# Routing a mixture-of-experts layer in another tile order: prompt tile 0, the sample tile, prompt tile 1

## The chip, the cores and the metric

The kernel runs on one core of a Trainium2 chip. It is one inference step of a two-layer hybrid decoder: a prompt group of 256 tokens and a sample group of 8 sequences with 8 tokens each, 320 tokens in all, in float32. The metric is the device time of one execution in microseconds (us). A core has five engines with a queue each: TensorE (PE, matrix products; its weight loads are shown as PEld), VectorE (DVE), ScalarE (ACT), GpSimd (POOL) and SyncE (SP, which here only issues DMAs). They meet through semaphores.

## The reference, cut to what matters

Each layer is a pair of mixers, whose outputs are projected back to width 1024 and added to the residual, followed by this block (`x` is the normalised residual):

```python
def hier_moe(x, p):
    xf = x.reshape(bt * t, dm)
    g_logits = (xf @ p['router_g']) + p['router_g_b']          # 4 groups
    g_idx = jnp.argmax(g_logits, axis=-1)
    e_logits = (xf @ p['router_e'] + p['router_e_b']).reshape(n, 4, 4)
    e_in = jnp.take_along_axis(e_logits, g_idx[:, None, None], axis=1)[:, 0]
    top_v, top_i = lax.top_k(e_in, 2)                           # 2 of the group's 4 experts
    top_w = jax.nn.softmax(top_v, axis=-1) * g_w
    ...
    hid = silu(x @ w_gate) * (x @ w_up)                         # 16 experts, 1024 -> 256
    y = (hid * gates) @ w_down                                  # 256 -> 1024
```

`yp + hier_moe(rmsnorm(yp))` and the same for the samples is what the changed part computes the beginning of: projection, norm, logits, choice, and the place of every token in its expert.

## The kernel before, in words

The 320 tokens lie in three tiles: tiles 0 and 1 are the prompt (128 rows each), tile 2 is the samples (64 rows); `ROWS = (P, P, NB * NS)`. `moe_block` runs once for each of the two layers, and only its first stage, up to the first expert product, is touched. In that stage each tile goes through the same steps, which pass between the engines:

1. PE: `project(t, h)` multiplies the mixers' output by the output weights, half `h` of 512 columns, in `n_parts` products of 128x512 (8 in layer 0, 6 in layer 1; `ahead` says how many are already done). For the samples, `project_samples(first, end)` does both halves of a part side by side in bank 4. The semaphore `done` counts finished halves.
2. DVE: `add(t)` adds the product to the residual (L1815), half by half; semaphore `added`.
3. ACT: square with row sum (L1736), square root (L1739); DVE: reciprocal in `mean(t)` (L1820); ACT: the scaled rows `xn` (L1741), which are also written to DRAM as `x_rows` (L1743) for later gathers.
4. PE: `turn_rows(t)` transposes the residual (L1439); DVE: `apply_gain(t)` copies it out with the norm's gain (L1827).
5. PE: `logits(t)` (L1447), DVE: `logits_out(t)` (L1835), PE: `logits_back(t)` (L1456).
6. DVE: `choose` and `mark`, a chain of short instructions (L1873 to L1905) that finds group and experts. Tiles 0 and 1 go through it together, tile 2 after them.
7. PE: `places` counts tokens of earlier tiles in each expert (L1463), DVE: `place` turns counts into one-hot slots `Sf` (L1910, L1913).
8. PE: `gather_first(t)` collects the rows of the first pair of experts, 8 products of 128x128 for each tile (L1470); DVE: `first_turned(h)` copies them out (L1840). Meanwhile DVE computes slot codes up to `L` (L1943), and PE multiplies them (L1608) to the table of row numbers `idx` (L1949), from which POOL starts the gathers of the later pairs (L1383).
9. PE: `up(0, 0, KC)`, the first expert product (L1499), 32 records, ends the stage. Seven more pairs of experts follow.

PE, DVE and ACT each take their instructions in the order in which the code is written; there is no planner. `keep_clock_up(bank, n, cols)` (L182) issues `n` products whose result nobody reads. SP waits for `done` to reach 6, then loads the next experts' weights into the room of the output weights (L135, L142), and piece by piece follows PE after that (L1263).

## Time and profile before

| | |
|---|---|
| median of 3 runs | 589.82 us (589.1 to 590.4) |
| profiled execution, its own time | 589.97 us |
| its span, first to last instruction | 587.9 us |
| PE busy | 565.3 us, 96% |
| DVE, ACT, POOL busy | 42%, 26%, 12% |
| mean granted TensorE clock | 0.991 |
| stage in layer 0, first projection to first expert product | 114.60 to 157.97 us |
| stage in layer 1 | 430.68 to 471.47 us |

A time in the trace is read from the span's start. The span ends about 2 us short of the execution's own time. In a timeline row the first number is the start, the second the duration of the merged instructions, `xN` the number of records (a float32 product is two records, a transpose one), and the brackets give idle time of the engine before the row and who ended it. Neighbouring PE records overlap by their pipeline depth, so the next row's start says more of the pace than the duration. The busy share counts every matmul record, useful or not.

### The profile page before, as it was taken

What the parts mean: (1) busy time and instruction counts of PE and PEld (TensorE: products, weight loads), DVE (VectorE), ACT (ScalarE), POOL (GpSimd) and SP (SyncE); (2) the same over time, 40 slices, a digit from 0 to 9 for tenths busy, and PEclk for the clock granted to TensorE, in tenths of its full rate; (3) what the DMA queues carried; (4) which work ended last, traced back from release to release, by engine and by line L of the source; (5) the groups of instructions that cost most, each with busy time, mean ns of one, the idle gap of its engine ahead of it and who ended that gap; (6) DMA issues with size and microseconds to landing.
All of it is one profiled execution on the core that took longest, in us unless ns stands there. A gap on an engine that the chain in (4) does not pass through costs nothing. (4 is left out here: it accounts for less than half of the span.)

```text
span 587.9 us, 8565 instructions
## 1 busy us (share of the span) xinstructions
PE 565.3 (96%) x3454; PEld 314.5 (53%) x3454; DVE 249.7 (42%) x595; ACT 154.6 (26%) x327; POOL 70.7 (12%) x114
## 2 busy tenths in 40 slices
PE   6999999999989999999999999999999899999994
PEld 5677876543633333337877555667644643333331
DVE  6999783224642211154542514260113742221146
ACT  6132195121301011034245104254003300101113
POOL 5900800000101210000100001000000021120000
PEclk9999999999899999999999999999999989999998
DMA  8994999896999999899899998999699999999972
GB/s 326 418 348 73 225 402 381 366 413 290 364 359 414 422 420 419 353 356 385 345 414 320 412 405 309 316 347 423 253 400 417 392 350 402 423 418 422 384 239 91
DMA packets 39930, 208.95 MB, mean 355 GB/s; under 512 B 12819, under 2 KB 14547, under 8 KB 23920
## 3 DMA queue, kind: packets, MB, share of 16 engines
q1 hardware_dynamic: 30416, 169.93, 74.2%
q0 software_dynamic: 7872, 34.53, 16.3%
q10 hardware_dynamic: 1600, 3.90, 1.7%
q8 instruction: 30, 0.49, 0.3%
q14 instruction: 12, 0.10, 0.0%
HBM read 198.77 MB, written 43.74 MB: 412 GB/s over the span
## 5 line engine op out<-in xcount | busy, mean ns | idle before, releaser
L1499 PE MATMUL bank<-arena 128*64 128x512 f32 x264 | 87.0, 611 | 0.2 <-DVE arena L1840 0.2
L1499 PE MATMUL bank<-ring,arena 128*64 128x512 f32 x232 | 76.1, 614 | 0.6 <-DVE arena L1849 0.5
L2315 PE MATMUL bank<-arena,ring 128*128 128x320 f32 x256 | 71.6, 434 | 0.0
L2315 PEld LDWEIGHTS bank<-arena,ring 128*128 128x128 f32 x256 | 48.0, 190 | 21.4 <-issue 1.6
L1499 PEld LDWEIGHTS bank<-arena 128*64 128x64 f32 x264 | 24.4, 140 | 32.8 <-issue 32.6
L1420 PE MATMUL bank<-ring,arena 128*128 128x512 f32 x92 | 40.3, 594 | 1.0 <-PEq L455 0.6
L1530 PE MATMUL bank<-arena 128*64 128x512 f32 x136 | 39.8, 594 | 0.7 <-ACT arena L1754 0.7
L577 PE MATMUL bank<-xnT,ring 128*128 128x320 f32 x144 | 39.5, 434 | 0.5 <-DVE xnT L896 0.5
L1974 DVE COPY arena<-bank 128x512 f32<-128x512 f32 x14 | 9.7, 692 | 68.3 <-PE bank L1530 68.3
L1530 PE MATMUL bank<-ring,arena 128*64 128x512 f32 x120 | 36.1, 593 | 0.7 <-ACT arena L1754 0.7
L1499 PEld LDWEIGHTS bank<-ring,arena 128*64 128x64 f32 x232 | 21.7, 140 | 26.2 <-issue 26.1
L577 PEld LDWEIGHTS bank<-xnT,ring 128*128 128x128 f32 x144 | 27.1, 190 | 11.6 <-DVE xnT L896 0.7
L1752 ACT ACTIVATE arena<-bank 128x256 f32<-128x256 f32 x16 | 6.1, 384 | 95.6 <-PE bank L1499 95.6
L1968 DVE TENSOR_TENSOR arena<-arena,bank 128x256 f32<-128x256 f32 x16 | 6.7, 421 | 55.2 <-ACT arena L1752 55.2
L1420 PEld LDWEIGHTS bank<-ring,arena 128*128 128x128 f32 x92 | 17.2, 190 | 22.7 <-issue 22.7
L1849 DVE TENSOR_TENSOR arena<-bank,small 128x512 f32<-128x512 f32 x28 | 18.0, 686 | 21.7 <-PE bank L1481 21.6
L1757 ACT COPY arena<-bank 128x512 f32<-128x512 f32 x16 | 9.4, 586 | 65.0 <-PE bank L1530 65.0
L1391 POOL DMA_INDIRECT y_rows<-arena x12 | 12.1, 1007 | 107.2 <-DVE arena L1974 107.2
L1530 PEld LDWEIGHTS bank<-arena 128*64 128x64 f32 x136 | 12.4, 136 | 20.7 <-issue 20.1
L2371 PE MATMUL bank<-ring,arena 128*128 128x512 f32 (+1 forms) x64 | 21.2, 489 | 0.0
L1736 ACT ACTIVATE arena<-resid 128x1024 f32<-128x1024 f32 (+1 forms) x6 | 6.3, 1058 | 54.8 <-DVE resid L1815 54.8
L1530 PEld LDWEIGHTS bank<-ring,arena 128*64 128x64 f32 x120 | 11.3, 136 | 16.2 <-issue 15.8
(451 smaller groups left out, 849.5 us busy)
## 6 DMA issues: line engine op xcount, KB each, us to landing
arena<-in_w_moe SPq DMA_DIRECT2D x50, 1024.0 KB, 15.6
ring<-in_w_moe SPq DMA_DIRECT2D x44, 1024.0 KB, 14.4
arena<-in_stream_b SPq DMA_DIRECT2D x4, 2560.0 KB, 14.5
out_o_d_old<-in_cache_d_g POOLq DMA_DIRECT2D x1, 8448.0 KB, 29.8
arena<-in_stream_a SPq DMA_DIRECT2D x4, 2048.0 KB, 10.1
out_o_d_old<-in_cache_d_g POOLq DMA_DIRECT2D x1, 7680.0 KB, 40.6
out_o_d_old<-in_cache_d_g SPq DMA_DIRECT2D x1, 4608.0 KB, 37.7
ring<-in_w_out_even SPq DMA_DIRECT2D x2, 2048.0 KB, 11.9
```

The costliest lines, as they stand in the source:

```text
L577: last = nc.tensor.matmul(bank(name)[:, 0:TOK], lhs(k), c.xnT[:, k, :], start=(k == 0), stop=(k == KC - 1))
L1391: pool.indirect_dma_start(out=x["y_rows"], out_offset=bass.IndirectOffsetOnAxis(ap=scatter_idx[:, j:j + 1], axis=0), in_=yo_of(j), in_offs ...
L1420: last = nc.tensor.matmul(c.bank[2 * t + h][:, :], parts[q][:, t * P:(t + 1) * P], where[q][:, h * 512:(h + 1) * 512], start=(q == 0), sto ...
L1499: last = nc.tensor.matmul(c.bank[2 + j % 2][half, :], xgT[:, j % 2, q, half], w[i][q // 4][:, q % 4, :], start=(q == 0), stop=(q == KC - 1))
L1530: last = nc.tensor.matmul(c.bank[4 + h][half, :], hidT[:, j % 2, f, half], w[i][:, f, h * 512:(h + 1) * 512], start=(f == 0), stop=(f == 1))
L1736: nc.scalar.activation(xn[0:rows, t], c.resid[0:rows, t], ACT.Square, accum_out=c.stat[0:rows, t:t + 1]).then_inc(sq_ok, 1)
L1757: nc.scalar.copy(yo_of(j)[:, 0:512], c.bank[4][:, :]).then_inc(yo_a, 1)
L1849: v.tensor_tensor(xgT[:, j % 2, 4 * h:4 * h + 4, :], c.bank[h][:, :].rearrange("p (k r) -> p k r", k=4), c.gains[:, gain, 4 * h:4 * h + 4] ...
L1968: v.tensor_tensor(hid[:, j % 2], sg[:, j % 2], c.bank[2 + j % 2][:, FF:2 * FF], ALU.mult).then_inc(hid_ok, 1)
L1974: v.tensor_copy(yo_of(j)[:, 512:D], c.bank[5][:, :]).then_inc(yo_b, 1)
L2315: last = nc.tensor.matmul(bank(name)[:, 0:TOK], w[:, k, i * P:(i + 1) * P], xnT[:, k, :], start=(k == 0), stop=(k == KC - 1))
L2371: last = nc.tensor.matmul(bank(f"v{2 * t + n}")[:, 0:m], xnT[:, k, t * P:(t + 1) * P], wv[:, k, c0:c0 + m], start=(k == 0), stop=(k == KC ...
```

## The change

The order of the tiles becomes 0, 2, 1 (`ROUTED`), and all semaphore counts follow it. PE issues tile 0's two halves, then the samples' projection with tile 0's transposes and logits amid it, then tile 1's projection with tile 2's transposes, logits and the `places` of tiles 0 and 2 amid it. Tile 1's transposes go to the banks as before, tile 2's to banks 4 and 7. The first half of tile 1 is transposed before its last product, the second half after it, with three `keep_clock_up` products on both sides. On DVE `choose`, `mark` and `place` are done for one tile at a time: three chains where there were two. The gathers of tiles 0 and 2 come after the projection, tile 1's last. `first_turned(1)` moves behind `idx`. SP's first piece in layer 0 waits for `first_pe` 3 and `rows_out` too.

```diff
+ROUTED = (0, 2, 1)
+TURN_BANKS = ((0, 1), (2, 3), (4, 7))
@@ SP
             if layer == 0:
                 sp.wait_ge(first_out, 32)
-                sp.wait_ge(first_pe, 2)
+                sp.wait_ge(rows_out, 16)
+                sp.wait_ge(first_pe, 3)
@@ PE
             project(0, 0)
             project(0, 1)
-            project(1, 0)
+            project_samples(0, 2)
             turn_rows(0)
-            project(1, 1)
+            project_samples(2, 4)
             pe.wait_ge(ld, ROUTER_LOADS)
             logits(0)
-            project_samples(0, 1)
-            turn_rows(1)
+            project_samples(4, n_parts - 1)
             logits_back(0)
-            project_samples(1, 2)
+            project_samples(n_parts - 1, n_parts)
+            project(1, 0, 0, 2)
+            turn_rows(2)
+            project(1, 0, 2, 4)
+            logits(2)
+            project(1, 0, 4, 5)
+            logits_back(2)
+            project(1, 0, 5, n_parts)
+            project(1, 1, 0, 3)
+            pe.wait_ge(tri_ok, 1)
+            pe.wait_ge(sel_ok, 2)
+            places((0, 2)).then_inc(pos_pe, 1)
+            project(1, 1, 3, n_parts - 1)
+            turn_rows(1, (0,))
+            project(1, 1, n_parts - 1, n_parts)
+            c.keep_clock_up(c.bank[0], 3, 256)
+            turn_rows(1, (1,))
+            c.keep_clock_up(c.bank[0], 3, 256)
             logits(1)
-            project_samples(2, 3)
+            pe.wait_ge(S0_ok, 2)
+            pe.wait_ge(xn_ok, 2)
+            gather_first(0, 0, 2)
             logits_back(1)
...
+            gather_first(0, 2, KC)
+            gather_first(2, 0, 4)
             c.keep_clock_up(c.bank[0], 2, 256)
-            pe.wait_ge(sel_ok, 2)
-            places((2,))
+            pe.wait_ge(sel_ok, 3)
+            places((1,))
             for u in range(3):
                 last = nc.tensor.matmul(c.bank[7][:, 64:80], ones, m["sum"][:, u, :], start=(u == 0), stop=(u == 2))
             last.then_inc(pos_pe, 1)
-            pe.wait_ge(S0_ok, 2)
+            gather_first(2, 4, KC)
+            pe.wait_ge(S0_ok, 3)
             pe.wait_ge(xn_ok, 3)
-            gather_first(2)
+            gather_first(1)
@@ DVE (choose, mark and place now take one tile)
             add(0)
             mean(0)
             apply_gain(0)
-            add(1)
-            logits_out(0)
-            mean(1)
-            apply_gain(1)
...
+            logits_out(0)
+            choose(0)
+            mark(0)
+            add(2)
+            mean(2)
+            apply_gain(2)
+            logits_out(2)
+            choose(2)
+            mark(2)
+            place(0)
+            place(2)
+            add(1)
+            apply_gain(1)
+            mean(1)
             logits_out(1)
-            choose(0, 2)
-            mark(0, 2)
+            choose(1)
+            mark(1)
...
             first_turned(0)
-            first_turned(1)
 
             dve.wait_ge(idx_pe, 1)
             v.tensor_scalar(m["idx"].bitcast(U32), ...).then_inc(idx_ok, 1)
+            first_turned(1)
```

PE in layer 0, in the middle of the stage, before: the line with 64x512 is the samples' projection (L1428), L1439 a transpose, L1447 and L1456 the logits and their way back, L1463 the counts, L1470 the gather.

```order
L1420 MATMUL bank<-ring,arena 128x512 x8
L1447 MATMUL bank<-xnT,arena 20x128 x8
L1428 MATMUL bank<-ring,arena 64x512 x2
L1439 MATMUL bank<-ident,resid 128x128 x8
L1456 MATMUL bank<-small,arena 128x20
L1428 MATMUL bank<-ring,arena 64x512 x2
L1447 MATMUL bank<-xnT,arena 20x128 x8
L1428 MATMUL bank<-ring,arena 64x512 x2
L1456 MATMUL bank<-small,arena 128x20
L1428 MATMUL bank<-ring,arena 64x512 x8
L1463 MATMUL bank<-arena 128x16 x3
```

The same place after, where the lines have moved on by 3 or 4 (L1432 is the samples' projection, L1443 a transpose, L1423 tile 1's projection):

```order
L1451 MATMUL bank<-xnT,arena 20x128 x8
L1432 MATMUL bank<-ring,arena 64x512 x6
L1460 MATMUL bank<-small,arena 128x20
L1432 MATMUL bank<-ring,arena 64x512 x2
L1423 MATMUL bank<-ring,arena 128x512 x2
L1443 MATMUL bank<-ident,resid 128x64 x8
L1423 MATMUL bank<-ring,arena 128x512 x2
L1451 MATMUL bank<-xnT,arena 20x64 x8
L1423 MATMUL bank<-ring,arena 128x512
L1460 MATMUL bank<-small,arena 64x20
L1423 MATMUL bank<-ring,arena 128x512 x6
L1467 MATMUL bank<-arena 128x16 x3
```

What stood after the whole of tile 1's projection now stands amid it, and the transposes that come after the samples' projection are the samples' own, three instructions behind its end.

PE in layer 0, end of the stage, before (L1599 is the count of all tiles, L1608 the row numbers, L182 `keep_clock_up`):

```order
L1439 MATMUL bank<-ident,resid 128x64 x8
L1470 MATMUL bank<-arena 128x128 x2
L1447 MATMUL bank<-xnT,arena 20x64 x8
L1470 MATMUL bank<-arena 128x128 x2
L1456 MATMUL bank<-small,arena 64x20
L1470 MATMUL bank<-arena 128x128 x8
L182 MATMUL bank<-resid,ident 128x256 x2
L1463 MATMUL bank<-arena 128x16 x3
L1599 MATMUL bank<-arena 128x16 x3
L1470 MATMUL bank<-arena 128x128 x8
L1608 MATMUL bank<-arena 128x16 x12
L1499 MATMUL bank<-arena 64x512 x16
```

And after, from the last projection on:

```order
L182 MATMUL bank<-resid,ident 128x256 x3
L1443 MATMUL bank<-ident,resid 128x128 x4
L182 MATMUL bank<-resid,ident 128x256 x3
L1451 MATMUL bank<-xnT,arena 20x128 x8
L1474 MATMUL bank<-arena 128x128 x2
L1460 MATMUL bank<-small,arena 128x20
L1474 MATMUL bank<-arena 128x128 x10
L182 MATMUL bank<-resid,ident 128x256 x2
L1467 MATMUL bank<-arena 128x16 x3
L1598 MATMUL bank<-arena 128x16 x3
L1474 MATMUL bank<-arena 128x128 x12
L1608 MATMUL bank<-arena 128x16 x12
```

Eight unread products stand there instead of two, and between the counts and the row numbers there are twelve gather products instead of eight.

DVE in layer 0 before, from tile 0's gain (L1827) on; L1815 is the addition of tile 1:

```order
L1827 TENSOR_TENSOR xnT<-bank,small 128x4x128 x2
L1815 TENSOR_TENSOR resid<-bank,resid 128x512 x2
L1835 COPY arena<-bank 128x128
L1820 RECIPROCAL stat<-stat 128x1
L1827 TENSOR_TENSOR xnT<-bank,small 128x4x128 x2
L1861 CAST arena<-arena 128x256
```

And after, from the reading of tile 0's logits (L1871) to the samples' addition (L1816) :

```order
L1871 SCALAR_TENSOR_TENSOR arena<-bank,stat,arena 128x16
L1874 MAX arena<-arena 128x8
L1875 MAX_INDEX arena<-arena 128x8
L1876 CAST arena<-arena 128x1
L1877 TENSOR_SCALAR arena<-arena 128x16
L1878 TENSOR_TENSOR arena<-arena 128x16
L1879 MAX arena<-arena 128x8
L1880 MAX_INDEX arena<-arena 128x8
L1881 CAST arena<-arena 128x2
L1887 TENSOR_TENSOR arena<-arena 128x16 x2
L1890 TENSOR_TENSOR arena<-arena 128x16
L1816 TENSOR_TENSOR resid<-bank,resid 64x512 x2
```

The samples' addition, which PE's transposes wait for, now stands behind this whole chain of choice for tile 0.

## Rows read from the trace of the kernel before

**Rows 1.** The page, part 1: engine, busy us, share, instructions.

```profile
PE 565.3 (96%) x3454; PEld 314.5 (53%) x3454; DVE 249.7 (42%) x595; ACT 154.6 (26%) x327; POOL 70.7 (12%) x114
```

**Rows 2.** Timeline of PE, layer 0: start, us, line, operation, records, idle before.

```profile
114.60 13.97 PE L1420 MATMUL bank<-ring,arena 128*128 128x512 f32 x32 [0.60 <-PEq L455]
128.41 1.04 PE L1439 MATMUL bank<-ident,resid 128*128 128x128 f32 x8
129.28 7.03 PE L1420 MATMUL bank<-ring,arena 128*128 128x512 f32 x16
136.25 0.63 PE L1447 MATMUL bank<-xnT,arena 128*20 128x128 f32 x16
...
138.75 0.30 PE L1456 MATMUL bank<-small,arena 128*128 128x20 f32 x2
...
146.12 0.22 PE L1463 MATMUL bank<-arena 128*128 128x16 bf16 x3 [0.57 <-DVE arena L1905]
146.26 1.08 PE L1428 MATMUL bank<-ring,arena 128*64 128x512 f32 x4
...
148.85 0.70 PE L1439 MATMUL bank<-ident,resid 64*128 64x64 f32 x8 [0.42 <-DVE resid L1815]
...
151.37 2.05 PE L1470 MATMUL bank<-arena 128*128 128x128 f32 x16
153.26 1.03 PE L182 MATMUL bank<-resid,ident 128*128 128x256 f32 x4
...
155.35 2.05 PE L1470 MATMUL bank<-arena 64*128 64x128 f32 x16 [0.76 <-DVE arena L1913]
157.37 0.44 PE L1608 MATMUL bank<-arena 128*128 128x16 bf16 x12
157.97 8.63 PE L1499 MATMUL bank<-arena 128*64 128x512 f32 x32 [0.16 <-DVE arena L1840]
```

**Rows 3.** Timeline of PE, layer 1.

```profile
456.25 2.79 PE L1428 MATMUL bank<-ring,arena 128*64 128x512 f32 x12
460.22 0.22 PE L1463 MATMUL bank<-arena 128*128 128x16 bf16 x3 [1.17 <-DVE arena L1905]
...
471.47 8.78 PE L1499 MATMUL bank<-ring,arena 128*64 128x512 f32 x32 [0.16 <-DVE arena L1840]
480.19 1.09 PE L1481 MATMUL bank<-ident,arena 128*128 128x128 f32 x8
...
486.51 3.65 PE L1499 MATMUL bank<-arena 128*64 128x512 f32 x16
```

**Rows 4.** Timeline of DVE, layer 0.

```profile
125.26 0.16 DVE L1820 RECIPROCAL stat<-stat 128x1 f32<-128x1 f32 x1 [2.82 <-ACT stat L1739]
129.05 1.29 DVE L1827 TENSOR_TENSOR xnT<-bank,small 128x512 f32<-128x512 f32 x2 [3.62 <-PE bank L1439]
...
147.39 1.41 DVE L1815 TENSOR_TENSOR resid<-bank,resid 64x512 f32<-64x512 f32 x2 [0.36 <-PE bank L1428]
...
151.55 0.21 DVE L1873 SCALAR_TENSOR_TENSOR arena<-bank,stat,arena 64x4 f32<-64x4 f32 x1 [0.68 <-PE bank L1456]
...
154.06 0.17 DVE L1905 TENSOR_TENSOR arena<-arena 64x16 bf16<-64x16 f32 x1
...
154.92 0.38 DVE L1913 TENSOR_TENSOR arena<-arena 128x128 f32<-128x128 f32 x1
```

**Rows 5.** Windows of 3 us: busy by engine, then PEclk, the granted clock.

```profile
158.00:161.00 3.00, 3.00 (x8) 1.06 (x10) 1.73 (x11) 0.00 (x0) 1.17 (x2) 0.50 1.03 434
472.00:475.00 3.00, 3.00 (x10) 1.19 (x8) 1.23 (x10) 0.00 (x0) 1.72 (x2) 0.50 0.84 341
```

**Rows 6.** Layer 1: first gather, by POOL.

```profile
472.98 1.10 POOL L1383 DMA_INDIRECT arena<-x_rows,arena  x1 [3.82 <-DVE arena L1949]
```

**Rows 7.** DMAs issued from 464.0 to 464.5 us: KB, us to landing.

```profile
x_rows<-arena ACTq DMA_DIRECT2D x1, 256.0 KB, 7.0
```

## What was predicted before the changed kernel ran

> **What bounds the kernel now.** I read the page's busy shares first: PE is busy for 565.3 of 587.9 us, 96% [rows 1], so a changed stage is paid for on PE unless PE waits there. Then PE's timeline through the two routing stages. In layer 0 PE waits 0.57 us for the choice of tiles 0 and 1 (L1905), 0.42 for the samples' addition (L1815), 0.76 for the last slots (L1913) and 0.16 for the first gained rows (L1840), 1.9 us in all [rows 2]. In layer 1 the same kind of waits are 1.17 and 0.16 [rows 3], and a third like layer 0's 0.76, some 2.1 us. That is all that hiding the chain can win as waits. Third, the granted clock: it stands at 0.50 from 158 to 161 us and from 472 to 475 us [rows 5], the lower of its two levels, 1.2 instead of 2.4 GHz. Both falls come right behind the same place: the samples' gather of 64 rows, which PE waited 0.76 us for, and twelve tiny products (L1608). The first expert product runs into them and takes 8.63 us in layer 0 and 8.78 in layer 1 [rows 2, 3]. Later the same work of 16 records takes 3.65 us with its drain [rows 3], so 3.5 of pace, and 32 records would be 7.1 with drain 7.2. The falls cost 1.4 us in layer 0 and 1.6 in layer 1, 3.0 together; half of twice 3.2 us at half speed gives the same size.
>
> So two accounts are moved by the change: the length of the stage up to the start of the first expert product, and the clock behind it.
>
> **Prices.** From starts of neighbouring rows: a 128x512 product 0.86 us (13.81 us for 16); eight transposes 0.87, four 0.45; the samples' eight 0.64 from a duration of 0.70 less overlap [rows 2]. A part of the samples' projection 0.87 in a run (2.79 less drain, for 3) [rows 3], 1.0 alone; logits about 0.56, their way back about 0.22, from 0.63 and 0.30 less overlap; a tile's gather 1.89 (151.37 to 153.26), so 0.24 a product [rows 2]. A `keep_clock_up` product of 256 columns is half of a 512 one, 0.43; the row's 1.03 for two [rows 2], which ends where a wait ends, bounds it at 0.52 from above. On DVE one chain of choice and marking is 2.68 us (151.55 to 154.23), the samples' addition 1.41, two gains 1.29, one slot instruction 0.38 [rows 4].
>
> **What is added outright.** Products nobody reads: eight instead of two in layer 0 (order, end of the stage) and eight instead of four in layer 1, where the old code had two more at the samples' turn. At 0.43 each that is 2.6 and 1.7 us. All other PE work is the same in number. So even without any wait the stage would be 2.6 - 1.9 = 0.7 us longer in layer 0 and 0.4 shorter in layer 1: the stage as such has next to nothing to win, and every new wait is a loss.
>
> **Walk through layer 0.** PE starts at 114.60. Eight products to 121.5, two sample parts, tile 0's transposes, two parts: 126.2. The logits need the gained rows. The reciprocal of tile 0 starts at 125.26 [rows 4]; before, the transposes were later than that, now it is what DVE's gains stand behind: 125.4 + 1.29 = 126.7. New wait 0.6. Then logits, three parts, way back, one part, two products of tile 1: 133.1. Here PE wants to transpose the samples. Their addition stands behind tile 0's choice on DVE: logits back at 130.3, copy and semaphores 0.3, 130.55 + 2.68 + 1.41 = 134.6. New wait 1.5, the largest one. From there PE has work: transposes 0.64, two products, logits (0.1 wait for ACT's and DVE's norm), one product, way back, six products, counts at 143.9 (the samples' choice ends at 141.5, in time), four, half a transposition, one: 148.8. Before, the projection ended at 147.3 (146.26 + 1.08). So +1.5.
>
> The tail, from there to the first expert product, was 157.97 - 147.34 = 10.6. Now on PE: three unread 1.3, half the transposes 0.45, three unread 1.3, logits 0.56, two gather products 0.5, way back 0.3, ten gather products 2.4, two unread 0.9, counts 0.2, four and eight gather products 2.85, row numbers 0.4, 0.2 of wait for the first gained half: 11.4. The DVE chain in it (way back at 4.5 us, choice 2.7, counts waiting for PE until 7.9, slots 0.6, codes 1.9, gained half 0.65) ends at the same 11.4: the two are balanced, and neither can be shortened alone. Tail +0.8. The same addition made for the old order comes out 0.2 too long in either layer, so I take that off: layer 0 is **+2.0 us**.
>
> **Walk through layer 1.** Six parts instead of eight leave fewer products to hide the same DVE chains. PE at 444.0 waits 0.6 for tile 0's gains, at 449.2 waits 1.5 for the samples' addition (DVE: 446.5 + 2.7 + 1.4), and at 460.1 another 0.3 for tile 1's first half, because two slot pairs (1.1 us) and an addition (0.7) are ahead of it on DVE. Projection ends at 461.8; before it was 459.0 (456.25 + 2.79) [rows 3]: +2.8. The old tail was 471.47 - 459.04 = 12.4, with the wait of 1.17 in it; the new one is 11.4 as above: -1.0. Less 0.2: **+1.5 us**. Stages together: +3.5 us.
>
> **The clock.** In the new tail no short stretch looks like the old one: the samples' gather is cut in two with other work around, the 128-row gather of tile 1 follows the other products without a wait, and the rest is filled with unread 128x256 products. The nearest rows for a stretch that keeps the clock are layer 1's at 460.22, with a wait of 1.17 us before it and two unread products behind [rows 3], where the clock stayed up. I take it that both falls go: **-3.0 us**; the ends are 0 (they stay) and -3.0 (there is nothing more to win, the clock is up elsewhere).
>
> The Trainium skill, "TensorE: Matmul & The Clock Gate", in the table "Why this matters for your kernels", lays a clock drop in mid-kernel to long gaps without matmuls. This trace does not agree: the longest gap before either fall is 0.76 us. By that page the unread products would be pure cost and the sum +3.5 us; that result is rival B's.
>
> **Edits at nothing.** ACT's square, root and copy of each tile (some 2.8 us from addition to written rows) lie beside PE's products; only tile 0's is met by the 0.6 wait above. SP's load of the next experts waits for the last projection, 1.5 and 2.8 us later; those weights serve the third pair, over 20 us on. The first piece in layer 0 moves by some 3 us and serves the fourth pair. `first_turned(1)` behind the row numbers is needed only at the fifth part of the first expert product. The first gather by POOL starts 1.1 us after the row numbers (472.98) and the transposes that need it come at 480.19 without a wait [rows 3, 6], so it takes at most 7.2 us; now both the rows' write and the row numbers end later. Write: tile 1's rows are scaled at 465.8 in layer 1, and landing took 7.0 us [rows 7], so about 473, against the row numbers at 473.3. Cover is left, but little, since the first expert product is 1.6 us shorter.
>
> **Sum.** +3.5 - 3.0 = +0.5 us on the profiled execution's own 589.97, so 590.5; that execution lies 0.15 above the median of 589.82, so about **590.4 us** in terms of the runs. Below 0.2% (1.2 us) nothing can be told from no change: the forecast is "the same, if anything a little slower".
>
> The page "TensorE: Matmul & The Clock Gate" of the Trainium skill, section "Architectural detail: the array is 16× 32×32, not 1× 128×128", says that VectorE takes its queue strictly in order. The trace agrees as far as it shows (L1815 of the samples starts only when the slots are written, 147.39). Were it otherwise, the addition would slip ahead of the choice and the two waits of 1.5 would go, giving 587.4.
>
> **Rivals.**
> - *B, the clock falls all the same* in one stage or both, because the chip counts the new filling as little as the old. For: transposes and narrow products are still much of the tail. Against: rows of layer 1 at 460. Price 1.5 for one, 3.0 for both: 591.9 to 593.4, slower. It is decided by the clock right behind the first expert product's start.
> - *C, the fall moves* to the new wait of 1.5 us and the samples' transposes behind it. For: the wait is longer than any that stands before a fall now. Against: full 128x512 products on both sides. Projections would run at half speed for some 3.2 us: +1.5, 591.9.
> - *D, a late transfer*: the first gather of layer 1 lands after the shortened first expert product. Against: POOL's bound of 7.2 us. Price 0 to 1.5: 590.4 to 592.
> - *E, faster*: the new chains on DVE overlap better than my sum, so the waits of 0.6 and 1.5 are halved in both layers (-2.1): 588.3. Against: each link has its own row.
> - That the change does not do what it says: excluded by the order, which shows two tiles' work amid the last projection.
>
> **Chances.** Forecast 0.55 (own range 589.4 to 591.6), B 0.17, C 0.08, D 0.08, E 0.12. Faster by over 0.2% (below 588.6): E's better half and more, 0.08, and a tail of the forecast, 0.05, with what the clock may give beyond my 3.0: 0.15 in all. Slower (above 591.0): B, C, most of D, and a quarter of the forecast, 0.40. Same: 0.45. Range for 8 in 10: 588.5 to 593.0.
>
> **What would show it.** Right: PE waits of about 0.6 before L1451 and 1.5 before L1443 in both layers; the first expert product starting near 160.0 in layer 0, taking 7.2 us; the granted clock at 1.00 from 158 to 163 us and around 474. Wrong: clock of 0.50 there (B) or amid L1423 (C), a wait at L1485 of layer 1 (D), or a first expert product that starts before 159 (E).

## The result and the profile after

| | before | after |
|---|---|---|
| median of the timed runs | 589.25 us (12 runs, 586.91 to 591.0) | 591.28 us (12 runs, 590.53 to 592.8) |
| profiled execution, its own time | 589.97 us | 590.57 us |
| its span | 587.9 us | 588.5 us |
| mean granted TensorE clock of it | 0.991 | 0.995 |

The ratio after / before is 1.0043, with a 95% interval of 1.0025 to 1.0061. The change makes the kernel 0.4% slower, about 2 us, beyond the 0.2% below which nothing can be told.

The page of the changed kernel, part 1, answers to [rows 1]:

```profile
PE 566.5 (96%) x3474; PEld 316.1 (54%) x3474; DVE 252.8 (43%) x611; ACT 154.5 (26%) x327; POOL 76.7 (13%) x114
```

Its PE timeline in layer 0 answers to [rows 2]. The first number is the start, the second the duration:

```profile
113.86 7.11 PE L1423 MATMUL bank<-ring,arena 128*128 128x512 f32 x16 [0.57 <-PEq L455]
...
126.01 0.63 PE L1451 MATMUL bank<-xnT,arena 128*20 128x128 f32 x16 [0.28 <-DVE xnT L1828]
...
133.89 0.71 PE L1443 MATMUL bank<-ident,resid 64*128 64x64 f32 x8 [1.27 <-DVE resid L1816]
...
148.22 1.46 PE L182 MATMUL bank<-resid,ident 128*128 128x256 f32 x6
...
155.23 1.13 PE L182 MATMUL bank<-resid,ident 128*128 128x256 f32 x4
...
159.80 7.09 PE L1503 MATMUL bank<-arena 128*64 128x512 f32 x32
```

And in layer 1, answering to [rows 3]:

```profile
430.98 8.82 PE L1423 MATMUL bank<-ring,arena 128*128 128x512 f32 x20 [0.41 <-PEq L2247]
...
451.02 0.71 PE L1443 MATMUL bank<-ident,resid 64*128 64x64 f32 x8 [1.29 <-DVE resid L1816]
...
461.93 1.46 PE L182 MATMUL bank<-resid,ident 128*128 128x256 f32 x6
...
473.49 7.09 PE L1503 MATMUL bank<-ring,arena 128*64 128x512 f32 x32
480.81 1.09 PE L1485 MATMUL bank<-ident,arena 128*128 128x128 f32 x8 [0.23 <-DMA arena<-x_rows,arena]
```

To be seen are the two waits that the new order makes in each layer (0.28 and 1.27 in layer 0), the first expert product that takes 7.09 us in both layers where it took 8.63 and 8.78, and one small wait at L1485 that was not there: the first gather of layer 1 now lands a little late. DVE's timeline shows what the longest wait stands behind:

```profile
129.81 0.22 DVE L1869 SCALAR_TENSOR_TENSOR arena<-bank,stat,arena 128x4 f32<-128x4 f32 x1 [2.74 <-PE bank L1460]
...
132.44 1.40 DVE L1816 TENSOR_TENSOR resid<-bank,resid 64x512 f32<-64x512 f32 x2
```

DVE idles 2.74 us until tile 0's logits come back, and only then, behind the 2.6 us chain of tile 0's choice, adds the samples, whose products had been ready (PE goes on to tile 1 at 130.64). The granted clock in the stretches of [rows 5] (last three numbers: clock, DMA share, GB/s) is now full:

```profile
158.00:161.00 3.00, 3.00 (x33) 2.28 (x33) 2.69 (x9) 0.00 (x0) 0.00 (x0) 1.00 1.02 426
472.00:475.00 3.00, 3.00 (x32) 2.11 (x32) 2.68 (x9) 0.00 (x0) 0.00 (x0) 1.00 1.03 433
```

The two executions divide into five stretches, cut at the first projection and the first expert product of each layer:

| stretch, us | before | after | difference |
|---|---|---|---|
| up to layer 0's stage | 114.60 | 113.86 | -0.74 |
| stage of layer 0 | 43.37 | 45.94 | +2.57 |
| from there to layer 1's stage | 272.71 | 271.18 | -1.53 |
| stage of layer 1 | 40.79 | 42.51 | +1.72 |
| from there to the end | 116.43 | 115.01 | -1.42 |
| span | 587.9 | 588.5 | +0.60 |

A negative difference means less time after. The first row is not the change's; a second pair of executions, below, has -0.02 there and 1.5 in all.

### The profile page after: what moved, and what is told of

Same layout as the page of the kernel before. It is cut to its first block and busy times, and to the rows that moved or that the text cites. A ratio compares the mean times of both kernels' runs of the same rounds, so it can differ in the third digit from the quotient of the medians.

```text
span 588.5 us, 8625 instructions
## 1 busy us (share of the span) xinstructions
PE 566.5 (96%) x3474; PEld 316.1 (54%) x3474; DVE 252.8 (43%) x611; ACT 154.5 (26%) x327; POOL 76.7 (13%) x114
## 5 line engine op out<-in xcount | busy, mean ns | idle before, releaser
L1503 PE MATMUL bank<-arena 128*64 128x512 f32 x264 | 85.4, 598 | 0.0
L1503 PE MATMUL bank<-ring,arena 128*64 128x512 f32 x232 | 74.4, 598 | 0.5 <-DVE arena L1850 0.5
L1423 PE MATMUL bank<-ring,arena 128*128 128x512 f32 x92 | 42.8, 605 | 1.0 <-PEq L455 0.6
L1534 PE MATMUL bank<-arena 128*64 128x512 f32 x136 | 39.8, 594 | 0.7 <-ACT arena L1755 0.7
L1534 PE MATMUL bank<-ring,arena 128*64 128x512 f32 x120 | 36.1, 593 | 0.7 <-ACT arena L1755 0.7
L577 PEld LDWEIGHTS bank<-xnT,ring 128*128 128x128 f32 x144 | 27.1, 190 | 11.6 <-DVE xnT L896 0.7
L1423 PEld LDWEIGHTS bank<-ring,arena 128*128 128x128 f32 x92 | 16.3, 189 | 19.9 <-issue 19.5
L1394 POOL DMA_INDIRECT y_rows<-arena x12 | 12.1, 1006 | 107.2 <-DVE arena L1963 107.2
L1534 PEld LDWEIGHTS bank<-ring,arena 128*64 128x64 f32 x120 | 11.4, 136 | 16.2 <-issue 15.8
```

Of the source, the lines that this page charges most:

```text
L577: last = nc.tensor.matmul(bank(name)[:, 0:TOK], lhs(k), c.xnT[:, k, :], start=(k == 0), stop=(k == KC - 1))
L1394: pool.indirect_dma_start(out=x["y_rows"], out_offset=bass.IndirectOffsetOnAxis(ap=scatter_idx[:, j:j + 1], axis=0), in_=yo_of(j), in_offs ...
L1423: last = nc.tensor.matmul(c.bank[2 * t + h][:, :], parts[q][:, t * P:(t + 1) * P], where[q][:, h * 512:(h + 1) * 512], start=(q == 0), sto ...
L1503: last = nc.tensor.matmul(c.bank[2 + j % 2][half, :], xgT[:, j % 2, q, half], w[i][q // 4][:, q % 4, :], start=(q == 0), stop=(q == KC - 1))
L1534: last = nc.tensor.matmul(c.bank[4 + h][half, :], hidT[:, j % 2, f, half], w[i][:, f, h * 512:(h + 1) * 512], start=(f == 0), stop=(f == 1))
```

## A second profile of either kernel

Both kernels were run once more, unchanged, to see which of the differences stay.

> The changed kernel once more, for a second profile. Its 12 runs have a granted clock of 0.995 at 590.6 and at 592.1 alike, so something besides the clock differs. Theory: it is the wait for the first gather in layer 1, 0.2 us in the first profile; a slower execution at the same clock shows 1 us or more there. Rival: the stages themselves differ in length, with the wait as before.

> The kernel before once more, for a second profile. Its runs fall into groups by clock: 0.988 at 590.5 to 591.3, 0.991 at 589.0 to 590.2, 0.994 and 0.995 at 587.1 to 587.8. Theory: the groups have three, two and one or no fall of the clock in the routing tails and elsewhere, 1.6 us each, and the stages have the same length in all of them (43.4 and 40.8 us up to the first expert product). Rival: the groups differ in waits, and the clock follows.

Measured: 591.04 and 589.57 us, spans 589.0 and 587.5. The changed kernel's first expert products:

```profile
160.21 7.09 PE L1503 MATMUL bank<-arena 128*64 128x512 f32 x32
...
474.00 7.09 PE L1503 MATMUL bank<-ring,arena 128*64 128x512 f32 x32
```

The old kernel's, and its windows just behind them, where the clock is again at the lower level for some 3 us:

```profile
157.64 8.53 PE L1499 MATMUL bank<-arena 128*64 128x512 f32 x32
...
471.08 8.79 PE L1499 MATMUL bank<-ring,arena 128*64 128x512 f32 x32 [0.16 <-DVE arena L1840]
```

```profile
157.00:160.00 3.00, 2.85 (x19) 1.24 (x20) 2.40 (x12) 0.00 (x0) 0.80 (x1) 0.53 1.01 427
471.00:474.00 3.00, 2.92 (x8) 1.15 (x10) 1.85 (x11) 0.00 (x0) 1.10 (x2) 0.53 0.90 380
```

In the table's rows this pair has -0.02, +2.59, -1.39, +1.74 and -1.42: +1.50. The differences behind the first row repeat to 0.15 us; the start before the stage is what moves from one execution to the next. Of the changed kernel this execution settles neither account: it is 0.5 us longer than the first at a like clock, with 0.19 us at L1485 for 0.23 and stages of the same length (45.96 and 42.54 us), and it only starts 0.4 us later. What makes its executions above 592 us longer is open.

The old kernel was also run beside the experiments below, and its times go with their mean clock: of 53 such executions, 23 have 0.988 or 0.989 (590.35 to 591.33 us, mean 590.8), 22 have 0.991 (588.99 to 590.18, mean 589.5), one is between, and 7 have 0.994 or 0.995 (587.08 to 587.76, mean 587.4). The steps are 1.3 and 2.1 us; one fall costs 1.4 to 1.7 us by the first expert products (8.53 to 8.79 us against 7.09). Both profiled executions are of the 0.991 kind: the clock is low for some 3 us around the start of each first expert product, and once more at the very end, where PE has no work. The third fall of the 0.988 kind was not seen in a profile of the old kernel; profiles of four other kernels below have one of the same length at 14.5 to 15.2 us, far from any change. That the seven fastest had only one of the two falls is inferred from the clock, not shown.

## The unread products taken out

```diff
             project(1, 1, n_parts - 1, n_parts)
-            c.keep_clock_up(c.bank[0], 3, 256)
             turn_rows(1, (1,))
-            c.keep_clock_up(c.bank[0], 3, 256)
             logits(1)
```

> The changed kernel without the two groups of three unread products around the second half of tile 1's transposes (the two before the counts stay). Theory: they cost PE 2.6 us in each tail and buy only cover; without them the tail is set by DVE's chain from the last addition, so the first expert product starts 1.0 to 1.4 us earlier in each layer after the end of the projection, and the clock stays up because the gather is still cut in two: 2 to 3 us faster than the changed kernel (591.3), near 588.8. Rival: the unread products are what holds the clock; then it is at 0.50 behind the start of the first expert product and the time stays near 591.

Measured: 596.75 us (6 runs), ratio to before 1.0115 (1.0089 to 1.0141). Neither account gave the time. The stages were 45.21 and 41.81 us, only 0.7 shorter each than with the six, for the expected 1.0 to 1.4: two waits of 0.8 took their place, at L1443 for tile 1's addition and at L1451 for its gains. So 1.9 of the 2.6 us of unread products lay beside DVE's chain, and cost nothing. The clock stayed at 1.00 behind both stages, so these six are not what holds it. The loss is elsewhere, in layer 1:

```profile
471.86 7.09 PE L1503 MATMUL bank<-ring,arena 128*64 128x512 f32 x32
483.39 1.97 PE L1485 MATMUL bank<-ident,arena 128*128 128x128 f32 x8 [4.44 <-DMA arena<-x_rows,arena]
```

```profile
486.00:489.00 3.00, 2.55 (x6) 0.86 (x8) 2.90 (x12) 0.19 (x1) 0.99 (x1) 0.50 1.01 419
```

PE waited 4.44 us for the first gather, up to 483.39, and the clock stood at 0.50 from 482.2 on, for 10 us. The Trainium skill, "TensorE: Matmul & The Clock Gate", in the table "Why this matters for your kernels", lays drops of the clock in mid-kernel to long gaps between matmuls. This fall agrees with it. The falls of the old kernel, behind 0.76 us, do not.

The last two unread products were then taken out as well:

```diff
             gather_first(2, 0, 4)
-            c.keep_clock_up(c.bank[0], 2, 256)
```

> The changed kernel without any of its eight unread products in the tail (3, 3 and 2 of 256 columns). Theory of the prediction (unread products hold the clock up): with the last two gone as well, the granted clock falls behind the first expert product's start in at least one layer, as before the change, to 8.6 us for its 32 records. Rival: the order of the tail holds it, the gather of tile 1 in one run with full rows: the clock stays up at 158 to 161 us in layer 0, and its stage is 0.3 to 0.9 us shorter than with the two (45.21). In layer 1 either shows only up to the wait for the late gather (4.4 us without the six).

One execution: 592.54 us. Layer 0's stage was 44.76 us (115.30 to 160.06), with a wait of 0.37 at the counts in the products' place. The clock, behind layer 0's stage and in layer 1's tail:

```profile
158.00:161.00 3.00, 2.99 (x34) 2.40 (x35) 2.76 (x9) 0.05 (x1) 0.00 (x0) 1.00 1.01 421
466.00:469.00 3.00, 3.00 (x15) 2.77 (x14) 2.26 (x15) 1.30 (x2) 0.00 (x0) 0.50 1.04 429
```

Neither side has it whole. In layer 0 no unread product was needed. In layer 1 the clock fell, but at 465.7, right behind the two waits of 0.8, not at the expert product; there DVE's chain covers most of it, and the stage is 42.41 us against 41.81. The two products taken out would have come only behind the gather products at 466.1, after this fall, so their absence can't be its cause; the kernel without the six has the same two waits in the same place, and its profile has no fall there. The same program text up to that point thus shows the clock both ways.

## The old order with two unread products before its last gather

```diff
             last.then_inc(pos_pe, 1)
+            c.keep_clock_up(c.bank[0], 2, 256)
             pe.wait_ge(S0_ok, 2)
             pe.wait_ge(xn_ok, 3)
             gather_first(2)
```

> The kernel before with two unread products of 128x256 in the 0.76 us wait ahead of the last gather; nothing else. Theory A: the fall of the clock at the tail came in only a part of the executions of the kernel before (its 12 runs span 586.9 to 591.0, the changed kernel's 590.5 to 592.8), so the changed kernel wins less than 3.0 us by the clock on the median; with the wait filled the falls go in all executions, the start of the first expert product moves by 0.1 to 0.2 us a layer, and the runs lie close together near 587.2. Theory B: the changed kernel's extra 1.5 us on the medians come from its own slow executions; then this kernel falls and spreads as before, near 589.3. Theory C: filling one wait is not enough, the 64-row gather itself lets the clock fall: profile still at 0.50 in both layers, time 589.5 or above.

Measured: 588.31 us (12 runs), ratio 0.9977 (0.9961 to 0.9994). PE in layer 0:

```profile
153.32 1.11 PE L182 MATMUL bank<-resid,ident 128*128 128x256 f32 x4
154.36 2.05 PE L1470 MATMUL bank<-arena 64*128 64x128 f32 x16
156.34 0.46 PE L1609 MATMUL bank<-arena 128*128 128x16 bf16 x12
156.84 7.09 PE L1499 MATMUL bank<-arena 128*64 128x512 f32 x32
```

And the window around the start of layer 1's first expert product, at 468.91 here:

```profile
469.00:472.00 3.00, 3.00 (x16) 1.21 (x18) 1.67 (x11) 0.00 (x0) 1.29 (x2) 1.00 0.84 355
```

The two products stand where the wait of 0.76 was [rows 2], the stage keeps its 43.37 us (40.81 in layer 1), and in the profiled execution both falls are gone, the second by the clock of 1.00 in that window. So the change's gain by the clock is to be had there in one line, without moving a tile. In the median it is less: theory A had all executions near 587.2, and they lie from 586.34 to 590.09, nearly as wide apart as the old kernel's, with a mean clock of 0.990 to 0.993 in six of the twelve; the changed kernel's twelve have 0.993 to 0.996. Where the clock is lost in those six was not profiled. Even in the profiled execution the gain is less than two falls: the stretch behind layer 1's stage is 116.19 us, where 116.43 less 1.6 was due. DVE at the end of this kernel:

```profile
563.62 2.61 DVE L2020 SCALAR_TENSOR_TENSOR resid<-arena,resid 128x1024 f32<-128x1024 f32 x2 [0.71 <-DMA arena<-y_rows]
567.84 5.23 DVE L2020 SCALAR_TENSOR_TENSOR resid<-arena,resid 128x1024 f32<-128x1024 f32 x4 [1.61 <-DMA arena<-y_rows]
```

Before the change the same six instructions run without a wait:

```profile
567.08 7.87 DVE L2019 SCALAR_TENSOR_TENSOR resid<-arena,resid 128x1024 f32<-128x1024 f32 x6
```

They add the earlier pairs' rows, which SP reads back from DRAM behind all weights. PE runs about 4 us earlier here; the DMA engines, at 1.01 of their share from 480 to 550 us, do not. The reads land 10.3 to 13.8 us after their issue instead of 6.6 to 10.7 (7.8 to 11.1 in the old kernel's second profile), and 1.4 us of the 1.6 is given back. In the changed kernel the beginning of this shows (0.74 and 0.44). The chain of waits that ended last in the changed kernel runs through the rows' write and the first gather, and at the end through a write and a read of `y_rows`; these pieces have start, duration and what:

```profile
465.83 9.01 DMA x_rows<-arena
...
475.71 5.06 DMA arena<-x_rows,arena
...
551.33 8.28 DMA y_rows<-arena
...
561.45 12.38 DMA arena<-y_rows
```

In the page's part 4 that chain is 6% DMA after the change and had none of it before.

Whether the place in the queue is what delays the reads was tried by letting POOL issue them in layer 1:

```diff
+    def earlier_in(eng):
+
+        for i in range(2):
+            scattered(eng, i, y_scatters[i])
+        rows = x["y_rows"].rearrange("(t two) d -> t (two d)", two=2)
+        for t in range(3):
+            eng.dma_start(m["yp"][t][0:ROWS[t]], rows[t * P:t * P + ROWS[t], :]).then_inc(yp_in[t], 16)
@@ SP, where these lines stood before
-                if j == LAST - 2:
+                if j == LAST - 2 and layer == 0:
+                    earlier_in(sp)
@@ POOL, behind its last scatter
+            if layer == 1:
+                earlier_in(pool)
```

> The old order with the unread products in front of its last gather, as in the run before, and in layer 1 the three reads of y_rows (1.28 MB) are issued by POOL, behind its last scatter, instead of by SP behind the last weights. Theory: in that earlier run the saved clock of layer 1 was given back at the end, because the DMA queues work at 1.01 of their share from 480 to 550 us whatever PE does, and SP's reads stand behind the weights of the last pair: VectorE waited 0.7 and 1.6 us for them, the last products' sums stood behind its additions, and the last stretch of the span was 1.4 us longer than before's. On a queue of their own the reads land in under 9 us instead of 10.3 to 13.8, both waits go, and the stretch from the first expert product of layer 1 to the end is 115.0 us instead of 116.2: 587.1 in the median. Rival 1: the engines' bandwidth, not the order in the queue, is the limit: the reads land no earlier, or the last weights are late for PE instead: 588.3 or more. Rival 2: the longer end has nothing to do with the reads (the last clock fall came 5.6 us earlier in it): the waits go, the time stays at 588.3.

Measured: 590.45 us (11 runs), ratio 1.0016 (0.9998 to 1.0035), some 2 us worse than with SP. The reads landed no earlier, as the first rival had it:

```profile
565.18 2.61 DVE L2026 SCALAR_TENSOR_TENSOR resid<-arena,resid 128x1024 f32<-128x1024 f32 x2 [2.16 <-DMA arena<-y_rows]
568.80 5.23 DVE L2026 SCALAR_TENSOR_TENSOR resid<-arena,resid 128x1024 f32<-128x1024 f32 x4 [1.01 <-DMA arena<-y_rows]
```

The reads, issued at 555.54, landed 11.1 to 13.3 us later, and the last stretch grew to 117.4 us, 1.2 more than with SP; the rest of the 2 us is not in the two profiles. The last norm's gains (512 KB), which SP had issued behind the reads, here went ahead of them, at 545.24; that this does not matter was not tested. The Trainium skill, "DMA: Bandwidth & Descriptors", section "Issuing engines are not separate DMA queues", says that DMAs from any engine run on the same 16 engines, so that another issuer saves only the issuing; the trace agrees.

## The new waits taken away by order alone

The way back of tile 0's logits goes two parts earlier in layer 0, DVE adds tile 1's first half ahead of the slots, and in layer 1 the samples' steps stand two products further back (layer 0's keep their places):

```diff
-            project_samples(4, n_parts - 1)
+            project_samples(4, 5)
             logits_back(0)
-            project_samples(n_parts - 1, n_parts)
-            project(1, 0, 0, 2)
-            turn_rows(2)
+            project_samples(5, n_parts)
...
+            else:
+                project(1, 0, 0, 4)
+                turn_rows(2)
+                project(1, 0, 4, n_parts)
+                logits(2)
+                project(1, 1, 0, 1)
+                logits_back(2)
+                project(1, 1, 1, n_parts - 1)
...
@@ DVE
+            add(1, (0,))
             place(0)
             place(2)
-            add(1)
+            add(1, (1,))
```

> The changed kernel with the new waits amid the projection taken away by order alone: in layer 0 the way back of tile 0's logits three sample parts earlier, in layer 1 the samples' transposes two products later and their logits and the counts two later, and tile 1's first half added before the slots. Theory: the wait of 1.3 us for the samples' addition goes in both layers and nothing takes its place, tails unchanged: 2.4 to 2.6 us faster than the changed kernel, 588.8. Rival: the chain of choice is only moved and PE waits for it at the counts instead (over 0.8 us at the counts in layer 1): 1.2 us faster at most.

(The way back of tile 0's logits is two parts earlier, not three.) Measured: 589.17 us (12 runs), ratio to before 0.9992 (0.9976 to 1.0007), from 1.0043: some 3 us for the expected 2.4 to 2.6, which the two intervals allow. The samples' transposes in layer 0 and in layer 1:

```profile
134.61 0.71 PE L1443 MATMUL bank<-ident,resid 64*128 64x64 f32 x8
...
452.79 0.71 PE L1443 MATMUL bank<-ident,resid 64*128 64x64 f32 x8
```

The waits of 1.27 and 1.29 are gone, the stages 1.33 and 1.10 us shorter (44.61, 41.41), and no new wait stands at the counts. The profiled execution is the longest of its twelve, 591.21 us, so only its stages are used here. So these waits are paid, all but 0.2 us, and they follow from where the steps stand, not from the order of the tiles.

## Gather products in the place of unread ones

On top of that, the gathers of tiles 0 and 2 moved between tile 1's steps, where six unread products had been; tile 1's transposes went to banks 0 and 1, and four unread products stayed, three ahead of the counts and one ahead of the last gather:

```diff
-TURN_BANKS = ((0, 1), (2, 3), (4, 7))
+TURN_BANKS = ((0, 1), (0, 1), (4, 7))
...
-            c.keep_clock_up(c.bank[0], 3, 256)
-            turn_rows(1, (1,))
-            c.keep_clock_up(c.bank[0], 3, 256)
+            gather_first(0, 0, 4)
+            turn_rows(1, (1,))
+            gather_first(0, 4, KC)
             logits(1)
```

> As the kernel with the waits gone, and the six unread products around tile 1's transposes replaced by the gathers of tiles 0 and 2 (tile 1's transposes go to banks 0 and 1, so that the gather may start in bank 2 at once); three unread products ahead of the counts, one ahead of the last gather. Theory: the tail from the end of the projection to the first expert product is then DVE's chain alone, 10.0 us instead of 11.4, in both layers, and the clock stays up: another 2.5 us faster than the kernel with the waits gone, near 586.3, faster than the kernel before. Rival: with four unread products instead of eight the clock falls at the tail in a part of the executions, 587.5 to 589.5 with a wide spread.

Measured: 594.37 us (6 runs), ratio 1.0085 (1.0055 to 1.0114). The stages became 0.99 us shorter each, 43.62 and 40.42 us, where 1.4 had been expected. Then came a wait again:

```profile
481.89 1.09 PE L1485 MATMUL bank<-ident,arena 128*128 128x128 f32 x8 [4.26 <-DMA arena<-x_rows,arena]
```

with the clock low for 6.8 us behind it. POOL in this kernel:

```profile
473.56 1.10 POOL L1386 DMA_INDIRECT arena<-x_rows,arena  x1 [5.33 <-DMA x_rows<-arena]
```

The gather starts only when tile 1's rows are written (8.9 us for 512 KB), and lands 8.3 us after its start. SP issues the next weight pieces, of 1 MB each, 0.7 us behind it. Over the kernels:

| pieces issued after the gather, us | its landing, us |
|---|---|
| 0.7 (this one), 0.7 (without the six) | 8.3, 8.5 |
| 0.9 (without any unread) | 6.4 |
| 1.5 (the changed kernel) | 5.1 |
| 2.2 (the old order, filled) | 4.2 |
| 3.9 (the old order) | 4.5 |
| only once it has landed (below) | 4.3 |

These kernels differ in more than this delay, so the table shows that the two go together, not that one sets the other. The last line is the test of it: SP waits for the gather before the spare pieces, and so before all that it has to issue behind them,

```diff
+                gathered(sp, 1)
                 load_piece(sp, FIRST_PIECES)
```

on the changed kernel and on this one.

> The changed kernel with one wait more on SP's queue in layer 1: the two spare pieces of weights (2 MB, loaded behind the rows' write and ahead of the first gather) are issued only when the first gather has landed. Theory: the rows' write of tile 1 lands in 6 to 7 us instead of 9, POOL's first gather waits for the row numbers and no more for the write, and PE's transposes of pair 1 have no wait. The changed kernel's profile has 0.23 us there, so 0.2 to 1 us is won over it, and the spread of its executions above 590.6 shrinks: 590.4. Rival: the two pieces then arrive too late in the fourth pair, PE waits for them and the time is 592 or above.

> The kernel whose gathers fill the tail, with the same wait on SP's queue. There the first gather waited for the rows' write, was then overtaken by the next pieces, landed after 9.6 us, PE waited 4.3 us in layer 1 and the clock fell behind that for 6.8 us. Theory: with the spare pieces out of the way the gather lands before the first expert product ends, both go, and the time is 594.4 - 4.3 - 3.4 = 586.7, below the kernel before. Rival: the gather is late because its own rows are written last, whatever else is in the queue: a wait of over 2 us stays, and the time stays above 590.

Measured: 599.26 us (6 runs), ratio 1.0159 (1.0126 to 1.0192), and 593.81 (6 runs), 1.0077 (1.0052 to 1.0102). Both theories failed in the time. In the second the gather's wait shrank, as its theory had it, and another came 80 us later, at a product that reads weights from the ring. The first row below is a window, with the DMA share behind the clock:

```profile
470.00:473.50 3.50, 3.50 (x19) 1.39 (x17) 0.87 (x6) 0.00 (x0) 1.21 (x2) 1.00 0.01 4
...
476.33 1.09 PE L1486 MATMUL bank<-ident,arena 128*128 128x128 f32 x8 [0.29 <-DMA arena<-x_rows,arena]
...
555.85 3.40 PE L1504 MATMUL bank<-ring,arena 128*64 128x512 f32 x8 [4.28 <-issue]
```

The first lost 4.9 us at the same line, in two waits of 1.30 and 3.61, far behind the fourth pair that its rival had named. The trace does not name what PE waited for there; that it was weights follows from the DMA engines, which stood idle for 3.5 us in the second (4 us in the first), work at 1.00 to 1.02 of their share from 480 to 550 us, and had that much less moved by then. What is kept from them early is missing late. The rows' write did not gain by it (8.7 and 8.9 us for 9.0 and 8.9).

The clock at these waits: around the one of 4.28 us it stood at 0.50 for 3.2 us, at the one of 3.61 us it stayed at 1.00.

So the late landing has to be covered on PE. In layer 1 the transposes of pair 1's rows were put behind pair 0's second product, as in layer 0:

```diff
-TURN_LATE = (True, False)
+TURN_LATE = (True, True)
```

> The kernel with the new order, the waits gone and gather products in the place of six unread ones (its stages were 43.62 and 40.42 us, against 43.37 and 40.79 before), with one change: in layer 1 the transposes of the second pair's rows stand behind pair 0's second product instead of ahead of it, as they do in layer 0 already. Theory: what that kernel lost in layer 1 (594.37 in the median) is the wait of 4.26 us for the gather that lands late, with the clock fall of 6.8 us behind it; the two down products (about 4 us) now cover the landing, and the hidden rows' transposes cost a wait of 0.7 to 1.2 us instead. 594.4 - 4.3 - 3.4 + 1 = 587.7. Rival: the wait only moves, since DVE and ACT reach pair 1's rows later, and the clock falls there: 590 or more.

Measured: 588.56 us (8 runs), ratio to before 0.9967 (0.9955 to 0.998), from 1.0085. PE in layer 1:

```profile
478.55 0.44 PE L1516 MATMUL bank<-ident,arena 128*128 128x128 f32 x2 [1.00 <-DVE arena L1968]
479.65 3.65 PE L1534 MATMUL bank<-ring,arena 128*64 128x512 f32 x16 [0.67 <-ACT arena L1765]
483.24 1.09 PE L1485 MATMUL bank<-ident,arena 128*128 128x128 f32 x8
...
485.20 3.65 PE L1503 MATMUL bank<-arena 128*64 128x512 f32 x16 [0.45 <-DVE arena L1860]
```

The 4.26 are gone, 1.0 and 0.45 came, and no fall stands there (the 0.67 was there before, 0.69 in the changed kernel). That is 0.9 us more than the 587.7 expected. This beats both kernels: 0.8% under the changed one by the two ratios, and 0.1% under the filled old order, which is less than the intervals can tell apart.

## Why the prediction came out as it did

- *Waits added*: right in place, high in size. 0.28 for the predicted 0.6 at the gains, 1.27 and 1.29 for 1.5 at the samples, and none for the 0.3 at the half turn of layer 1. Yet their ends, which DVE sets, came within 0.1 us of the walk, counted from the stage's start: 12.15 us for 12.1 and 20.0 for 20.0 in layer 0. PE merely got there later than summed, because a 128x512 product that is cut off from its run costs more than the 0.86 us priced: 1.06 alone (136.79 to 137.85), 1.91 for two (134.53 to 136.44). The shorter waits and the dearer products are one miss with two signs, and it leaves the stage as it was. The experiment without the large waits confirms their price.
- *End of the projection*: 34.4 us after the start in layer 0, +1.6 for the predicted +1.5; 30.95 in layer 1, +2.6 for +2.8.
- *Tail*: 11.6 us in both layers for the predicted 11.4; +0.95 for +0.8 and -0.87 for -1.0. DVE's chain and PE's work are balanced there only to 0.7 us: six unread products out bring that much of 2.6 us, so PE's part could be shortened alone by it.
- *The step that failed in size* is the correction at the end of either walk: "the same addition made for the old order comes out 0.2 too long", taken off twice. The new order's addition was not too long. Stages: +4.3 us for +3.5, 0.4 us of the miss from this correction, 0.2 from rounding both stages down behind it, and the rest in the tails (+0.3) and the ends of the projection (-0.1).
- *The clock*: the falls went, as predicted, and behind layer 0 brought 1.4 to 1.5 us. Together -2.8 to -2.95 for -3.0; in layer 1 the small wait of rival D (0.2 us) and DVE's waits at the end stand against it. But the reason given was only half right. The new filling was said to hold the clock: without the six, and in layer 0 without all eight, it held as well, in one profile each. What the old order lacked was anything in the wait of 0.76 before its last gather; there two products held it in the profiled execution. Nor is 0.76 us the longest gap before either fall, as the prediction says, but the nearest one: in layer 1 the 1.17 of [rows 3] stands 11 us ahead.
- *The sum*: +0.5 predicted, +1.5 in the pair of like executions. The other half us of the measured 2.0 lies between those two executions and the medians: the old kernel's is 0.3 above its median of twelve, the changed one's 0.2 below. Above its median stands an execution with both falls; in some others the old kernel has a better clock by itself, and there the change has less to win back. The prediction priced both falls by one profile and did not ask in how many executions they come.
- *The call*: the forecast was "the same, if anything a little slower", with 0.45 for the same and 0.40 for slower by over 0.2%. It is slower by over 0.2%, so the likelier side did not come, though 591.3 us for 590.4 lies inside the range. Added up from the prediction's own parts the two sides are about even (some 0.44 for slower, 0.42 for the same). Without the correction the sum would have been +0.9, three quarters of the way to the bound of 1.2.
- *Rivals*: B, C and E did not come. D came with 0.23 and 0.19 us in the changed kernel, and with 2.2 to 4.4 us in three kernels whose tail was shortened. For that rival the prediction had the mechanism right and two sizes wrong. It took the write's 7.0 us from [rows 7], where the last tile's rows are the samples' 256 KB; the last tile is now tile 1 with 512 KB, and took 9.0. And the gather's own landing, bounded by 7.2 us, came to 8.3 and 8.5 where SP issued new pieces 0.7 us behind it.
- *VectorE's order*: the prediction reads the samples' addition at 147.39 as starting only when the slots are written. Its row says otherwise: DVE was idle for 0.36 us and PE's last part released it [rows 4]. The changed kernel shows the order: the addition at 132.44 follows the chain of choice without a gap, its products long ready.

Left open: why the old tail loses the clock behind a wait of 0.76 us when longer ones, 1.17 us in layer 1 of the same kernel [rows 3], 1.27 in the changed one, and even 3.61 in the one with the pieces later, do not; which fall the old kernel is spared in its fastest executions; and where the filled old kernel loses the clock in the slower half of its own.

## What to carry to other kernels

When a reordering promises fewer waits and a better clock, price the two apart and ask whether the second is to be had alone: here two unread products in one wait of 0.76 us gave 0.23% in the median, and the reordering only added waits. Before you shorten a stage ahead of a stretch in which the DMA engines are full, look at which transfers start with it and which stand behind the whole load, since those do not move with PE. And carry a walk's correction over to a new order only if you know where it comes from.

## What the runs showed of the hardware

- The indirect gather of 128 rows landed in 4.3 us with no new load beside it, in 4.2 to 4.5 where weight pieces of 1 MB each followed 2.2 to 3.9 us later, in 5.1 where they followed after 1.5 us, and in 8.3 to 8.5 us where they followed after 0.7 us.
- The write of tile 1's rows in layer 1, 512 KB, took 8.7 to 9.6 us to land over the kernels with the new order; one of 256 KB in its place took 7.0 in the old one.
- Falls of the granted clock to 0.50 at the first expert product cost 1.4 to 1.7 us each and came in the old kernel behind a wait of 0.76 us amid narrow products, while a wait of 1.27 us amid full 128x512 products left the clock at 1.00. At waits over 4 us it stood low for 10 (4.44), 7 (4.26) and 3 us (4.28), and one wait of 3.61 us left it at 1.00.
